# Four cache pages side by side on 32 partitions each, in the decode attention of a hybrid layer

## The chip, the cores and the metric

The kernel runs on one core of a Trainium2 chip. The metric is the time on the device of one execution, in microseconds (us): 3503.11 us before the change, the median of three runs (3503.08 to 3503.35). The core has five engines with a queue of instructions each: PE (TensorE, matrix products), DVE (VectorE), ACT (ScalarE), POOL (GpSimd) and SP (SyncE, which here only issues transfers). Transfers between the chip's memory (HBM) and the on-chip memory of 128 partitions are carried out by 16 DMA engines as packets, one for each contiguous run of bytes. SP and ACT issue theirs to queues of their own (q1 and q10 in the profile), POOL its gathers by index to q0; the 16 engines serve all of these queues.

## What is computed

One layer of a hybrid decoder for two groups: a prompt of 1024 tokens (eight tiles of 128) and eight samples of one new token each. Each token goes through latent attention beside a short gated convolution, and then through a mixer that fetches 128 rows of 1024 numbers from each of two expert tables. All numbers are float32.

The part that the change touches is the attention of the samples over their past. Each sample has 2048 past keys, in 16 pages of 128 keys; a page table says where each page lies. A key has a latent of 256 numbers (`ckv`) and a rotary part of 64 (`krope`):

```
past_ckv = cache_ckv[l, page_table].reshape(dec_b, past, KV_RANK)
past_kr = cache_krope[l, page_table].reshape(dec_b, past, QK_ROPE)
keys_ckv = jnp.concatenate([past_ckv, ckv], axis=1)
keys_kr = jnp.concatenate([past_kr, kr], axis=1)
s = (einsum('bqhr,bkr->bhqk', q_lat, keys_ckv)
     + einsum('bqhp,bkp->bhqk', q_rope, keys_kr)) * SM_SCALE
p = softmax(where(mask, s, -inf))
o_lat = einsum('bhqk,bkr->bqhr', p, keys_ckv)
```

A sample's new token comes after all of its past, so the mask hides none of these keys, and neither the softmax nor the weighted sum depends on the order in which the keys stand.

## The kernel before

**Two streams.** The mixer is the long one. For each prompt tile, 128 slots are worked off in 32 groups of four: for every slot POOL issues two gathers (L1853), each fetching one 4 KB row of `expert_u` or `expert_v` for each of the 128 tokens, 512 KB in all, into one of eight places of `u_ring` or `v_ring`. DVE multiplies a `u_ring` place with the tokens (L1736), ACT applies a gelu (L1215) and makes weighted diagonal matrices (L1222), and PE adds up the `v_ring` rows (L924). POOL waits for a place to come free, by `u_free` and `v_free`, before it issues the next gather into it. Between two tiles ACT reloads `xn2_cur` with the next tile's tokens (L1235), in two DMAs that write 64 partitions each.

Around this, a plan written out at build time puts the stages of everything else, one or a few per group: the projections and the attention of later prompt tiles and then of the samples. The samples' stages lie in groups 193 to 249 of 256, 36 of them named `pages` (groups 201 to 230).

**The pages.** The 16 pages of a sample are worked off in four quarters of four. The stage `pages` n takes quarter q = n % 4 of sample b = n // 4:

- `page_turn` on PE waits until all DMAs of the quarter have landed (`pages_loaded[b % 2][q]`), then transposes the four pages, two blocks of latents (L861) and one of rotary keys (L862) for each, into PSUM; ACT and DVE copy them to `pages_T` (L1156, L1523, L1524).
- `page_scores` multiplies them with the queries of all samples (L839, L840), ACT copies the result (L1153), and `page_scores_turn` picks and turns sample b's scores (L852).
- Once a sample's four quarters are through, the softmax follows, and `page_values` (L878, L881, L883), two stages into the next sample, weighs the latents as they lie in their load buffer. Its end counts `page_pv`.

There are two sets of buffers. Odd samples use `work`, even ones `ckv_rows` and `ckvT` (free by then) for latents and `w_ukT` for rotary keys. In both, page n is the slab of 256 (or 64) numbers at place n, and its 128 keys lie on the 128 partitions.

**SP's queue.** SP issues in a fixed order: the latents of sample 0 early, during the stage before; then loads of the rope tables (`cos_t`, `sin_t`, 64 partitions each, L477 and L478), of weights and of the sample tokens (`x_t`, L458); then the rotary keys of sample 0; then both parts of samples 1 to 7. From sample 2 on it waits first for `page_pv` of sample b - 2, whose buffer it overwrites. For each page it reads the page number from the table (L533) and issues one DMA for latents (128 KB) and one for rotary keys (32 KB), both at L536. Then come the weights of the samples' remaining stages.

Of the kernel before, what the change touches and what calls it, by code (L numbers as in the profile page):

```python
# [26 lines left out]
P = 128  # L27
# [3 lines left out]
TILES = SEQ // P  # L31
# [8 lines left out]
KV = 256  # L40
# [31 lines left out]
QP = NPAGES // QUARTERS  # L72
# [188 lines left out]
def build(nc, a, out):  # L261

    with ExitStack() as ctx:
        def sb(name, shape, dt=F32):
            return ctx.enter_context(nc.sbuf_tensor(name, shape, dt))
# [44 lines left out]
        work = sb("work", [P, 5 * D])  # L310
# [41 lines left out]
        prompt_keys = [ckv_rows[:, :, :], ckvT[:, :, :].rearrange("p c (n r) -> p (c n) r", r=KV)]  # L352
        pages_kr = [w_ukT[:, :, :].rearrange("p h (n r) -> p (h n) r", r=ROPE),
                    work[:, NPAGES * KV:NPAGES * (KV + ROPE)].rearrange("p (n r) -> p n r", r=ROPE)]

        def page_rows(b, n):
            if b % 2:
                return work[:, n * KV:(n + 1) * KV]
            return prompt_keys[n // TILES][:, n % TILES, :]

        pages_T = rows_next[:, :, :].rearrange("p a b -> p (a b)")[:, 0:3 * 512].rearrange("p (c k) -> p c k", c=3)

        SPREAD = [W[0], W[1], W[2], W[3], W[4], mix_raw, o_lat, x_t[:, :]]
# [81 lines left out]
        def _(sp):  # L445
# [19 lines left out]
            r = 0  # L465
            for name in ("g_mix_norm", "g_q", "g_kv", "g_attn_out", "g_conv_out"):
                n = a[name].shape[1] // P
# [5 lines left out]
            def load_rope(u):  # L473

                after(sp, on.q_roped, UNITS[u][0])
                row, T = UNITS[u][0] * P, width(u)
                sp.dma_start(cos_t[:, 0:T], a["c_rope"][0, :, row:row + T]).then_inc(on.rope_loaded, 16)  # L477
                sp.dma_start(sin_t[:, 0:T], a["c_rope"][1, :, row:row + T]).then_inc(on.rope_loaded, 16)  # L478
# [53 lines left out]
            def load_page(b, n, what):  # L532
                page = sp.value_load(page_table_sb[0:1, b * NPAGES + n:b * NPAGES + n + 1], min_val=0,  # L533
                                     max_val=a["cache_ckv"].shape[1] - 1)
                for dst, src in what:
                    sp.dma_start(dst, a[src][0, bass.ds(page, 1)].rearrange("a k r -> k (a r)"))\  # L536
                        .then_inc(pages_loaded[b % 2][n // QP], 16)

            sp.wait_ge(on.olat_kept, TILES * H)  # L540
            sp.wait_ge(on.pages_table_loaded, 16)
            for n in range(NPAGES):
                load_page(0, n, [(page_rows(0, n), "cache_ckv")])
            load_rope(SAMPLE)
            load_unit_start(SAMPLE)
            for k in range(CONV, N_IN + WR):
# [5 lines left out]
            sp.wait_ge(on.conv_done, SAMPLE + 1)  # L552
            sp.wait_ge(on.conv_stored, 3 * 16)
            for n in range(NPAGES):
                load_page(0, n, [(pages_kr[0][:, n, :], "cache_krope")])
            for b in range(1, SB):

                if b >= 2:
                    sp.wait_ge(on.page_pv, b - 1)
                for n in range(NPAGES):  # L560
                    load_page(b, n, [(page_rows(b, n), "cache_ckv"), (pages_kr[b % 2][:, n, :], "cache_krope")])
            for k in range(N_IN + WR, PIECES):
                load_w(SAMPLE, k)

# [1387 lines left out]
```

## Time and profile before

| | |
|---|---|
| median of 3 runs | 3503.11 us |
| the profiled execution: time | 3499.09 us |
| the profiled execution: span from first to last instruction | 3497.3 us |
| mean granted TensorE clock, as a share of full speed | 0.842 |
| busy: PE, DVE, ACT, POOL | 71%, 65%, 23%, 65% |
| moved by DMA | 1279.47 MB, 366 GB/s on average |
| page stage (first to last `pages` stage) | about 2768 to 3158 us |

The page of the profile gives the busy time of each engine, the DMA queues with their packets, megabytes and share of the time of 16 engines, and the costliest lines. The view of windows gives the same sums for a stretch of time: busy time and count of instructions for each engine, the granted clock, the share of the DMA engines' time taken by packets, and the rate in GB/s. A share can come out slightly over 1, as the records of packets overlap a little. "Under 512 B", "under 2 KB" and "under 8 KB" count all packets below that size, the 4-byte ones that raise semaphores among them. SPq and ACTq are the queues of SP and ACT, where their DMAs are issued.

### The profile page before, as it was taken

The numbers are of one execution on the slowest core, as the hardware profiler recorded it, in microseconds if no ns is written. First come the engines' busy times: TensorE is split into PE (matmuls) and PEld (weight loads), VectorE is DVE, ScalarE is ACT, GpSimd is POOL, SyncE is SP. The second block draws the span as 40 slices with busy tenths as digits, with TensorE's granted clock in tenths as the row PEclk, the third lists the DMA queues.
The fourth block names the chain that finished last, engine by engine and source line by source line (L and its number), as shares of the span: only waits on it lengthen the run. The fifth ranks groups of instructions, "written<-read, shape, count | busy, mean of one in ns | idle before, by whom it ended". The sixth has DMA issues, their size and how long they took to land.

```text
span 3497.3 us, 38783 instructions
## 1 busy us (share of the span) xinstructions
PE 2499.0 (71%) x11520; PEld 1392.1 (40%) x11520; DVE 2279.7 (65%) x5456; ACT 812.6 (23%) x2057; POOL 2290.4 (65%) x2068
## 2 busy tenths in 40 slices
PE   7558775878764598777744978778656978776764
PEld 6425442645531264445311644445213534332321
DVE  3585586655688756657898466558796455554774
ACT  2112212232211212322112223322112122221111
POOL 0366575655657776676777767666676676657675
PEclk8779887999987799899877999889876798987777
DMA  6699999988999999999999999999999999999998
GB/s 237 224 399 363 347 410 334 388 313 298 372 351 372 370 404 371 352 366 412 409 371 372 397 392 349 331 374 410 405 371 379 388 387 370 368 323 394 411 409 338
DMA packets 368936, 1279.47 MB, mean 366 GB/s; under 512 B 59372, under 2 KB 77974, under 8 KB 353368
## 3 DMA queue, kind: packets, MB, share of 16 engines
q0 software_dynamic: 297216, 1082.26, 80.7%
q1 hardware_dynamic: 62324, 168.67, 12.6%
q10 hardware_dynamic: 9188, 26.05, 2.3%
q8 instruction: 95, 1.56, 0.2%
q14 instruction: 113, 0.93, 0.1%
HBM read 1262.31 MB, written 13.48 MB: 365 GB/s over the span
## 4 chain that ended last, share of the span: by engine, by line
DVE 37%; PE 30%; DMA 15%; issue 8%; ACT 4%; SPq 3%; POOL 2%; DVEq 0%; ACTq 0%; POOLq 0%
DVE u_ring L1736 15%; PE acc L924 9%; PE front L586 8%; DMA u_ring<-in_expert_u,pick_cur 7%; DMA v_ring<-in_expert_v,pick_cur 4%; PE front L802 3%; DVE si_u L1603 2%; SPq L536 2%; DVE sv L1602 2%; PE front L711 2%; DVE work L1603 2%; DMA w_ukT<-in_cache_krope 2%; POOL u_ring L1853 1%; DVE work L1602 1%; PE front L734 1%
## 5 line engine op out<-in xcount | busy, mean ns | idle before, releaser
L924 PE MATMUL acc<-v_ring,diag 128*64 128x512 f32 x4096 | 1161.5, 716 | 612.6 <-ACT diag L1222 352.9
L1853 POOL DMA_INDIRECT v_ring<-in_expert_v,pick_cur x1024 | 1133.2, 1107 | 606.1 <-PE acc L924 333.0
L1853 POOL DMA_INDIRECT u_ring<-in_expert_u,pick_cur x1024 | 1140.5, 1114 | 575.4 <-issue 295.1
L1736 DVE CUSTOM_DVE_ANT_0 u_ring<-u_ring,xn_cur 128x1024 f32<-128x1024 f32 x1024 | 1210.8, 1222 | 315.4 <-DMA u_ring<-in_expert_u,pick_cur 309.3
L924 PEld LDWEIGHTS acc<-v_ring,diag 128*64 128x64 f32 x4096 | 340.7, 163 | 1316.6 <-issue 856.9
L1222 ACT ACTIVATE diag<-ident,wgt 128x64 f32<-128x64 f32 x1024 | 272.3, 337 | 797.6 <-DVE wgt L1742 727.9
L586 PE MATMUL front<-work,w_ring 128*128 128x256 f32 (+2 forms) x1536 | 308.1, 343 | 31.0 <-DVE mo L1337 17.1
L586 PE MATMUL front<-mo,w_ring 128*128 128x256 f32 (+2 forms) x1536 | 300.5, 337 | 0.0
L586 PEld LDWEIGHTS front<-work,w_ring 128*128 128x128 f32 x1536 | 250.5, 200 | 83.0 <-issue 29.3
L1215 ACT ACTIVATE gelu<-dots 128x4 f32<-128x4 f32 x256 | 52.5, 205 | 962.9 <-DVE dots L1736 962.8
L586 PEld LDWEIGHTS front<-mo,w_ring 128*128 128x128 f32 x1536 | 255.3, 201 | 23.4
L802 PE MATMUL front<-w_ring,work 128*128 128x256 f32 (+1 forms) x512 | 119.0, 394 | 22.4 <-DVE work L1568 16.7
L1602 DVE MAX8 sv<-work 128x8 f32<-128x128 f32 (+1 forms) x252 | 72.6, 288 | 75.9 <-ACT work L1200 29.9
L802 PEld LDWEIGHTS front<-w_ring,work 128*128 128x128 f32 (+1 forms) x512 | 93.5, 185 | 52.8 <-DVE work L1568 18.5
L1523 DVE COPY rows_next<-front 128x512 f32<-128x512 f32 x32 | 22.1, 691 | 139.7 <-PE front L862 139.7
L1215 ACT ACT_TABLE_LOAD x81 | 103.9, 1283 | 1.5
L734 PE MATMUL front<-work,ckv_rows 128*128 128x128 f32 x560 | 80.3, 307 | 28.7 <-DVE work L1507 25.2
L734 PEld LDWEIGHTS front<-work,ckv_rows 128*128 128x128 f32 x560 | 74.8, 217 | 40.8 <-DVE work L1507 29.5
L1736 DVE DVE_READ_ACCUMULATOR2_ANT dots<- 128x1 f32 x1024 | 84.0, 82 | 0.0
L711 PE MATMUL front<-ckvT,rows_next 128*128 128x512 f32 (+3 forms) x176 | 74.1, 546 | 7.0 <-DVE q_ro L1424 5.9
L1493 DVE SCALAR_TENSOR_TENSOR work<-low_keys,small,front 128x512 f32<-128x512 f32 (+3 forms) x44 | 26.6, 635 | 70.6 <-PE front L712 70.6
L1603 DVE FIND_INDEX8 si_u<-sv,work 128x8 uint32<-128x128 f32 (+1 forms) x252 | 71.5, 284 | 0.6 <-issue 0.6
(303 smaller groups left out, 2374.6 us busy)
## 6 DMA issues: line engine op xcount, KB each, us to landing
w_ring<-in_w_pieces SPq DMA_DIRECT2D x112, 1024.0 KB, 8.4
u_ring<-in_expert_u,pick_cur POOLq DMA_INDIRECT x1024, 10.5
v_ring<-in_expert_v,pick_cur POOLq DMA_INDIRECT x1024, 9.7
x_t<-in_x_prompt SPq DMA_DIRECT2D x16, 512.0 KB
v_ring<-in_w_pieces SPq DMA_DIRECT2D x8, 1024.0 KB, 12.0
work<-in_cache_ckv SPq DMA_DIRECT2D x64, 128.0 KB, 7.9
xn_cur<-scratch ACTq DMA_DIRECT2D x14, 512.0 KB, 9.8
scratch_x<-rows_next ACTq DMA_DIRECT2D x8, 512.0 KB, 6.6
```

The costliest lines, as they stand in the source:

```text
L536: sp.dma_start(dst, a[src][0, bass.ds(page, 1)].rearrange("a k r -> k (a r)"))\
L586: last = nc.tensor.matmul(dst, w[:, k, c0:c0 + m], x_chunks(k // 4)[:, (k % 4) * T:(k % 4 + 1) * T], start=(k == 0), stop=(k == DC - 1))
L711: nc.tensor.matmul(dst, q_lat[:, c, h, :], ckvT[:, c, ks], start=(c == 0), stop=False)
L734: last = nc.tensor.matmul(F[4][:, c * P:(c + 1) * P], ckv_rows[:, j, c * P:(c + 1) * P], W[1][:, j * P:(j + 1) * P], start=(j == 0), stop= ...
L802: last = nc.tensor.matmul(dst, mixed[i][:, k * T:(k + 1) * T], w[:, k, :], start=(k == 0), stop=(k == DC - 1))
L924: last = nc.tensor.matmul(acc[rows, half, :], diag[:, s % RING, :], v_ring[:, s % RING, half * 512:half * 512 + 512], start=(s < 2), stop= ...
L1215: nc.scalar.activation(gelu[:, g * G:(g + 1) * G], dots[:, g * G:(g + 1) * G], ACT.Gelu).then_inc(on.gelu_done, 1)
L1222: nc.scalar.activation(diag[:, s % RING, :], ident2[:], ACT.Copy, scale=wgt[:, s:s + 1]).then_inc(on.diag_made, 1)
L1602: own(v.max(best, scores), held=True)
L1603: last = v.max_index(index[:, 8 * r:8 * r + 8], best, scores)
L1736: v.tensor_tensor_reduce(u_ring[:, slot, :], u_ring[:, slot, :], xn2_cur[:, block_of(r), :], 1.0, 0.0, ALU.mult, ALU.add, dots[:, g * G + ...
L1853: pool.indirect_dma_start(ring[:, slot, :], None, a[table][0], bass.IndirectOffsetOnAxis(ap=pick, axis=0)).then_inc(loaded[slot], 16)
```

## The change

A page of latents is 128 rows of 1 KB, one after the other in memory, and was written row by row to 128 partitions. Now four consecutive rows go to one partition: a page takes 32 partitions and the room of four slabs, and the four pages of a quarter lie side by side, page i of the quarter on partitions 32 i to 32 i + 31. The same is done with the rotary keys. The new `page_block` and `kr_block` give the places to write to; `page_rows` stays, and a slab that it gives now holds every fourth key of each of the four pages. Since latents and rotary keys are permuted alike, a quarter is used only when whole, and the order of keys doesn't matter, nothing else changes: not the readers, the number or order of DMAs, the waits, nor the buffers.

```diff
+        def page_block(b, n):
+
+            q, i = divmod(n, QP)
+            part = slice(i * P // QP, (i + 1) * P // QP)
+            if b % 2:
+                return work[part, q * QP * KV:(q + 1) * QP * KV]
+            rows = prompt_keys[q * QP // TILES][part, q * QP % TILES:q * QP % TILES + QP, :]
+            return rows.rearrange("p n r -> p (n r)")
+
+        def kr_block(b, n):
+
+            q, i = divmod(n, QP)
+            return pages_kr[b % 2][i * P // QP:(i + 1) * P // QP, q * QP:(q + 1) * QP, :].rearrange("p n r -> p (n r)")
...
                 for dst, src in what:
-                    sp.dma_start(dst, a[src][0, bass.ds(page, 1)].rearrange("a k r -> k (a r)"))\
+                    sp.dma_start(dst, a[src][0, bass.ds(page, 1)].rearrange("a (m j) r -> (a m) (j r)", j=QP))\
                         .then_inc(pages_loaded[b % 2][n // QP], 16)
...
-                load_page(0, n, [(page_rows(0, n), "cache_ckv")])
+                load_page(0, n, [(page_block(0, n), "cache_ckv")])
...
-                load_page(0, n, [(pages_kr[0][:, n, :], "cache_krope")])
+                load_page(0, n, [(kr_block(0, n), "cache_krope")])
...
-                    load_page(b, n, [(page_rows(b, n), "cache_ckv"), (pages_kr[b % 2][:, n, :], "cache_krope")])
+                    load_page(b, n, [(page_block(b, n), "cache_ckv"), (kr_block(b, n), "cache_krope")])
```

Here P is 128, QP 4 (pages in a quarter), TILES 8, KV 256.

## Rows read from the trace of the kernel before

**Rows 1.** The page: busy time, and two DMA queues (packets, MB, share).
```profile
PE 2499.0 (71%) x11520; PEld 1392.1 (40%) x11520; DVE 2279.7 (65%) x5456; ACT 812.6 (23%) x2057; POOL 2290.4 (65%) x2068
...
q0 software_dynamic: 297216, 1082.26, 80.7%
q1 hardware_dynamic: 62324, 168.67, 12.6%
```

**Rows 2.** Windows of the whole core, columns in the first line.
```profile
core 0: us, PE busy (x) PEld busy (x) DVE busy (x) ACT busy (x) POOL busy (x), PEclk, DMA share, GB/s
2492.00:2532.00 40.00, 21.73 (x70) 7.68 (x72) 36.48 (x95) 7.37 (x21) 27.75 (x25) 0.77 1.03 409
...
2635.00:2641.00 6.00, 2.95 (x8) 1.08 (x10) 5.55 (x16) 3.74 (x7) 4.47 (x6) 0.62 1.02 256
...
2761.00:2764.00 3.00, 0.36 (x2) 0.40 (x3) 1.23 (x2) 0.70 (x3) 2.39 (x3) 0.80 1.01 361
...
3085.00:3090.00 5.00, 3.53 (x26) 2.62 (x25) 1.03 (x2) 1.17 (x2) 0.00 (x0) 1.00 0.44 130
...
2768.00:3158.00 390.00, 312.83 (x1687) 151.98 (x1686) 194.75 (x409) 101.58 (x250) 255.46 (x224) 0.86 0.99 361
3158.00:3490.00 332.00, 203.82 (x892) 85.62 (x884) 212.33 (x515) 56.60 (x177) 229.81 (x219) 0.77 1.00 398
```

**Rows 3.** DMA queues, 2492 to 2532 us: packets, MB, share.
```profile
q0 software_dynamic: 4484, 16.32, 102.5%
```

**Rows 4.** DMA queues, 2456 to 2475 us (latents of sample 0).
```profile
DMA packets 3302, 7.52 MB, mean 396 GB/s; under 512 B 362, under 2 KB 1835, under 8 KB 3301
...
q0 software_dynamic: 1651, 6.01, 80.7%
```

**Rows 5.** DMA queues, 2996 to 3024 us (page stage).
```profile
DMA packets 5225, 11.00 MB, mean 393 GB/s; under 512 B 1738, under 2 KB 2904, under 8 KB 5224
...
q0 software_dynamic: 2608, 9.50, 86.8%
q1 hardware_dynamic: 2616, 1.49, 17.6%
```

**Rows 6.** Reload of xn2_cur: its issue, and DMA queues 2635 to 2641 us.
```profile
L1235 ACTq DMA_DIRECT2D xn_cur<-scratch x2: 605/613/621, 2630.4 to 2631.1; - x2
...
q0 software_dynamic: 221, 0.83, 55.1%
q10 hardware_dynamic: 197, 0.70, 46.8%
```

**Rows 7.** Rope tables: issue, and DMA queues 509.5 to 512.5 us.
```profile
502.66 0.58 SPq L478 DMA_DIRECT2D sin_t<-in_c_rope  x1
...
DMA packets 394, 1.08 MB, mean 360 GB/s; under 512 B 62, under 2 KB 153, under 8 KB 394
...
q0 software_dynamic: 271, 0.99, 93.1%
```

**Rows 8.** DMA queues, 2768 to 3158 us (the page stage).
```profile
q0 software_dynamic: 32899, 119.80, 81.2%
q1 hardware_dynamic: 34560, 18.89, 16.5%
q10 hardware_dynamic: 432, 1.57, 1.4%
```

**Rows 9.** Timeline of SP's queue (start, duration), two pages of sample 4.
```profile
2938.33 0.34 SPq L536 DMA_DIRECT2D ckv_rows<-in_cache_ckv  x1
...
2939.94 0.34 SPq L536 DMA_DIRECT2D ckv_rows<-in_cache_ckv  x1
```

**Rows 10.** Waits of PE, 2768 to 3158 us: total, times, longest.
```profile
PE front L861 <- DMA w_ukT<-in_cache_krope: 29.7, 9, 7.4
PE front L861 <- DMA work<-in_cache_krope: 16.0, 5, 7.4
```

## The prediction

> **What bounds the kernel now.** I read the page first: no compute engine is busy for more than 71% of the span, while the expert gathers take 80.7% of what 16 DMA engines have and the queue of SP and its like 12.6% more [rows 1]. Then the windows. Where nothing but gathers is under way the DMA share is 1.03 at 409 GB/s, the most that this kernel moves. The page stage (attention of the eight samples over their cache pages, 2768 to 3158 us) has a share of 0.99 but 361 GB/s, and after it the rate is 398. PE is busy for 313 of its 390 us, DVE for 195 [rows 2]. So the DMA engines are the bound, and in the page stage something makes them less productive. Every DMA microsecond added or saved there moves all that follows, as the gathers stay the bound to the end.
>
> Last I took the price of each kind of packet out of windows in which the DMA engines never idle, as (window x 16 engines) less what the others took.
> - Gathers alone: 40 us x 16 = 640 us of engine time for 16.32 MB, or 3984 packets of 4096 bytes: 0.161 us each [rows 3].
> - Key rows of sample 0 (1 KB packets, 128 partitions): 19 x 16 = 304, less 6.01 MB of gathers (1467 x 0.161 = 236), leaves 68 for 1835 - 362 = 1473 packets: 0.046 each [rows 4].
> - Page stage in full flow, 1 KB and 256 B packets mixed: 28 x 16 = 448, less 9.50 MB (2319 x 0.161 = 373), leaves 75 for 2616 packets of q1: 0.029 each [rows 5]. In the stage q1 has 34560 packets for 240 page DMAs, 144 a DMA (128 and 16 for the semaphore); a page (two DMAs) has 288, or 8.3 us of engine time [rows 8].
>
> **What the change does, part by part.**
> 1. *Fewer, larger packets.* A page of latents goes from 128 packets of 1 KB to 32 of 4 KB, its rotary keys from 128 of 256 B to 32 of 1 KB. At the wide prices a page would cost 32 x 0.161 + 32 x 0.046 = 6.6 us instead of 8.3; over 128 pages and 16 engines that is -1.7 x 8 = -13.6 us.
> 2. *Fewer partitions per DMA.* Each page DMA now writes 32 partitions instead of 128. No DMA of before does just that, but two kinds write 64, and both spoil the rate. The reload of `xn2_cur` (L1235, two DMAs of 64 partitions, 4 KB packets) [rows 6] drops it to 256 GB/s with the engines never idle [rows 2]: 6 x 16 = 96 us, less 0.83 MB of gathers (203 x 0.161 = 32.7), leaves 63.3 for 0.70 MB, 171 packets: 0.37 each, 2.3 times the wide price [rows 6]. The rope tables (64 partitions, 1 KB packets) cost 3 x 16 = 48, less 0.99 MB (242 x 0.161 = 38.9), 9.1 for 153 - 62 = 91 packets: 0.100 each, 2.2 times [rows 7]. An 8-row load of the sample tokens leaves 361 GB/s behind it [rows 2], so fewer partitions are at least no better. I bound a page between no penalty, 6.6 us, and the rope and reload prices, 32 x 0.37 + 32 x 0.100 = 15.0 us. The nearest rows are the 64-partition ones; as these were dense bursts and the page packets come thinner, I take a little over twice, 2.05 x 6.6 = 13.5 us. Against 8.3 that is +5.2 x 128 / 16 = +42 us (+54 at the upper price, +39 at exactly twice).
> The Trainium skill ("SBUF — State Buffer", "Door 1: The DMA port swizzle (why `[64,N]` ≈ `[32,N]`)") states that partitions 0 to 31 reach the same eight of the sixteen SBUF ports as 0 to 63, and 64 to 127 the other eight, so 32 rows go as slowly as 64. The trace agrees for 64 (0.37 against 0.161 us) and has no 32-row DMA; by the rule the sum is mine, without it only the -13.6 us of part 1 would stand. Its "DMA: Bandwidth & Descriptors" ("Why a DMA increments its semaphore by 16 and not by 1") has a DMA of 32 rows still spread over 16 engines; no row here shows one.
> 3. *Pages land sooner.* Queues take turns packet by packet: in full flow 2608 packets of the gathers' queue stand beside 2616 of q1 [rows 5]. A quarter (four pages) is 4 x 288 / 16 = 72 packets an engine, each behind a gather packet: 72 x (0.161 + 0.029) = 13.7 us. SP issues a page in 1.61 us, a quarter in 6.4 [rows 9]. After the change a quarter has 24 packets an engine (8 + 8 and 8 for semaphores), at the doubled price 4 x 13.5 / 16 + 24 x 0.161 = 7.3 us, near what SP needs to issue it. PE now waits for pages in 14 turns for 45.7 us [rows 10]; behind it the ring fills, the gathers stop, and slices like 3085 to 3090 move 130 GB/s [rows 2]. I expect most of these waits gone. What they are worth is the idle time of the DMA engines, not 45.7 us: 390 x 16 = 6240, less gathers 119.80 MB (29248 x 0.161 = 4709), page packets 34560 x 0.029 = 1002, q10's 1.57 MB (256 slow at 0.37 and 127 at 0.161, 115), instructions some 19, leaves 395 / 16 = 25 us [rows 8]. The stage after it, without pages, runs 2.7% under 409 GB/s [rows 2], which over 390 us is 10; so 15 us come back, between 0 and 22.
> 4. *No other step moves.* Same number of DMAs, instructions, semaphores and waits; the keys of a quarter are only permuted alike in latents and rotary keys. SP's issue is paid per DMA (0.33 us), so it stays at 1.61 us a page. The 16 latent DMAs of sample 0 stand in the 128 pages of part 2. PE and DVE keep their cover: 313 us of PE work in a stage of some 415.
>
> **The sum.** +42 - 15 = +27 us on the profiled execution's 3499.1 us, 3526; its median of runs is 4 us above, so 3530.
>
> **Rivals.**
> - *A, narrow writes cost double (forecast).* 3530; by its bounds +39 - 22 = +17 to +54 - 4 = +50, so 3520 to 3553.
> - *B, no penalty: faster.* The page DMAs alternate, two pages on the lower and two on the upper 64 partitions, and come thinner than a burst; if what is buffered absorbs the crowding, only parts 1 and 3 count: -13.6 - 15 = -29, 3474 (3465 to 3485). It decides the sign when a page costs less than 8.3 + 15 / 8 = 10.2 us, that is, under about 1.5 times the wide price. Against it: the rope burst brings a mere 128 KB, as one page does, and pays in full.
> - *C, half the penalty.* A page at 10 us: +14 - 15, 3502 (3495 to 3512).
> - *D, the packets don't merge.* If rows of 1 KB remained and only narrowed, a page would cost 2 x 8.3: +66 and no waits saved, 3569. Against: rows that are contiguous on both sides already move as 4 KB packets in the gathers.
>
> **How the numbers follow.** A 0.56, C 0.14, B 0.26, D 0.04. This kernel's measurement tells about 0.2%, 7 us, from no change. Slower: A, D and the upper fifth of C, 0.62; faster: B and a little of C, 0.28; same: 0.10. A's own range is 3520 to 3553. Eight in ten need A, C and half of B: 3474 to 3554 leaves out the lower half of B (0.13), D and a thin tail of A. Cases of both signs are in it, because the penalty for 32 partitions is read from 64-partition DMAs.
>
> **What will show it.** Packets of q1 in the page stage fall from 34560 to about a third (11520, 48 a DMA): right for part 1, and D is out. A window of the page stage with a DMA share over 1 and under 350 GB/s, where gathers and 4 KB page packets should give 400: A. The same window near 400 GB/s: B. Waits of PE L861 on page DMAs under 15 us: part 3. The page stage grows from 390 to about 415 us, and the stages before and after it keep their length. I am wrong if the stage shrinks, or if it grows while the DMA share falls below 0.95, for then something other than the DMA engines would set it.

## The result

After the change the kernel takes 3527.2 us, the median of its runs, beside 3503.2 us for the kernel before: the ratio is 1.0064, with a 95% interval of 1.0051 to 1.0078. It is 24 us slower. (One of the six runs of after, at 3613 us, was in a slower state, and the ratio leaves it out.) The profiled execution takes 3527.2 us, its span is 3524.7.

The windows of after, of the page stage, of the stage behind it, and of 20 us in the page stage. The columns are those of [rows 2].

```profile
core 0: us, PE busy (x) PEld busy (x) DVE busy (x) ACT busy (x) POOL busy (x), PEclk, DMA share, GB/s
3070.00:3090.00 20.00, 11.91 (x57) 5.29 (x55) 7.78 (x18) 4.65 (x10) 11.63 (x11) 0.91 1.04 286
2776.00:3190.00 414.00, 321.77 (x1689) 149.21 (x1688) 197.14 (x409) 101.59 (x250) 262.59 (x229) 0.84 1.03 343
3190.00:3520.00 330.00, 205.67 (x888) 87.24 (x884) 210.95 (x517) 59.24 (x180) 227.92 (x214) 0.76 0.99 396
```

The page stage has grown from 390 to 414 us, and it moves 343 GB/s instead of 361 although the DMA share has risen from 0.99 to 1.03 [rows 2]: the engines are busy all the time and get less done. The stage behind it is as fast as before (396 against 398).

The DMA queues of after in the page stage, 2776 to 3190 us (packets, MB, share):

```profile
q0 software_dynamic: 33259, 121.12, 84.6%
q1 hardware_dynamic: 11520, 18.89, 16.8%
q10 hardware_dynamic: 433, 1.57, 1.4%
```

The packets of q1 are 11520 for the same 240 DMAs and the same 18.89 MB, a third of the 34560 before [rows 8]: the rows did join to 4 KB and 1 KB. But a third of the packets takes more of the engines (16.8% of 414 us against 16.5% of 390).

The price of a page, as in the prediction, is the time of DMA engines that one page takes, summed over the 16. From 3070 to 3090 us of after:

```profile
q0 software_dynamic: 1072, 3.90, 70.0%
q1 hardware_dynamic: 1070, 1.80, 33.7%
q8 instruction: 1, 0.02, 0.4%
q14 instruction: 1, 0.01, 0.1%
```

20 x 16 = 320 us of engine time, less 952 gather packets at 0.161 (153) and 1.6 for q8 and q14, leaves 165 for 1.80 MB. A page is 0.164 MB, so this is 11.0 pages, 15.0 us each. By [rows 5] the same sum gives 8.2 before. The 27 windows of 20 us in this stage of after without idle engines lie between 13.4 and 16.4, with a median of 14.8 (a table further down has those of all runs).

The sum charges the whole loss to the pages, but the records show that the gathers bear part of it. A packet of q0 (those for semaphores included) takes 1.025 x 640 / 4484 = 0.146 us where gathers are alone [rows 3], 0.868 x 448 / 2608 = 0.149 in the page stage of before [rows 5], and 0.70 x 320 / 1072 = 0.209 in this window. The gathers are the same in both kernels.

The early latents of sample 0 alone, 2455 to 2472 us of after, answer to [rows 4]:

```profile
DMA packets 1620, 4.81 MB, mean 283 GB/s; under 512 B 459, under 2 KB 459, under 8 KB 1608
...
q0 software_dynamic: 809, 2.95, 63.0%
q1 hardware_dynamic: 810, 1.85, 40.9%
```

272 us, less 720 gather packets (116) and 12 weight packets of 8 KB (about 4), leaves 152 for 1.75 MB or 427 packets: 0.356 us for a 4 KB packet to 32 partitions, beside 0.161 for one of a DMA over 128 and 0.37 for the reload over 64 [rows 6]. For the 16 DMAs that is 182 us of engine time against 94 before, 5.5 us of the 8.2 by which the first transpose of the pages starts later (2791.4 us against 2783.2).

The waits of PE in the page stage of after (total, times, longest):

```profile
PE acc L938 <- DMA v_ring<-in_expert_v,pick_cur: 62.4, 21, 9.7
PE front L866 <- ACT low_keys L1167: 11.0, 3, 9.7
PE acc L938 <- ACT diag L1236: 5.7, 2, 4.6
PE front L875 <- DMA w_ukT<-in_cache_krope: 3.9, 2, 2.2
PE front L875 <- DMA work<-in_cache_krope: 3.0, 1, 3.0
```

L875 is L861 of before, L938 is L924. The waits for pages have fallen from 45.7 us [rows 10] to 6.9. In their place PE waits 62.4 us for the gathers, against this in the page stage of before:

```profile
PE acc L924 <- DMA v_ring<-in_expert_v,pick_cur: 12.5, 8, 3.4
```

### The profile page after: what moved, and what is told of

Its sections match the earlier page's. It is cut to its first block, busy times and chain, and to the rows that moved or that the text cites. A ratio compares the mean times of both kernels' runs of the same rounds, so it can differ in the third digit from the quotient of the medians.

```text
span 3524.7 us, 38783 instructions
## 1 busy us (share of the span) xinstructions
PE 2522.5 (72%) x11520; PEld 1394.0 (40%) x11520; DVE 2280.6 (65%) x5456; ACT 812.7 (23%) x2057; POOL 2294.4 (65%) x2068
## 4 chain that ended last, share of the span: by engine, by line
DVE 35%; PE 31%; DMA 18%; issue 8%; ACT 4%; POOL 4%; DVEq 0%; SPq 0%; ACTq 0%; POOLq 0%
DVE u_ring L1750 14%; PE acc L938 10%; DMA u_ring<-in_expert_u,pick_cur 9%; PE front L600 8%; DMA v_ring<-in_expert_v,pick_cur 7%; PE front L816 3%; POOL u_ring L1867 2%; DVE si_u L1617 2%; PE front L725 2%; DVE sv L1616 2%; DVE work L1617 1%; POOL v_ring L1867 1%; DVE work L1616 1%; PE front L748 1%; DVE work L1661 1%
## 5 line engine op out<-in xcount | busy, mean ns | idle before, releaser
L938 PE MATMUL acc<-v_ring,diag 128*64 128x512 f32 x4096 | 1195.0, 733 | 660.2 <-ACT diag L1236 336.5
L938 PEld LDWEIGHTS acc<-v_ring,diag 128*64 128x64 f32 x4096 | 348.0, 166 | 1387.1 <-issue 932.6
L1236 ACT ACTIVATE diag<-ident,wgt 128x64 f32<-128x64 f32 x1024 | 272.3, 337 | 793.3 <-DVE wgt L1756 727.9
```

The lines of the kernel that those rows point to most:

```text
L938: last = nc.tensor.matmul(acc[rows, half, :], diag[:, s % RING, :], v_ring[:, s % RING, half * 512:half * 512 + 512], start=(s < 2), stop= ...
L1236: nc.scalar.activation(diag[:, s % RING, :], ident2[:], ACT.Copy, scale=wgt[:, s:s + 1]).then_inc(on.diag_made, 1)
```

## The experiments

Two theories. T: packets of a DMA that writes a narrow range of partitions crowd on few destinations and hold up the engines, gathers included. R: the large page packets take every second turn from the gathers, and it is their lateness that costs the time. The price of a page, from windows in which the engines never idle, tells whether the narrow range costs engine time; the times tell whether that decides. The times need one remark. They come from five measurements, in each of which the kernel before ran too. In two, the first and that of e9 to e11, it takes 3501 to 3503 us. In the other three (e1 to e4, e5 to e8, e12), each on another chip, it took 3635 to 3640, with larger scatter. Only e9 to e11 test the time where the DMA engines are the bound; what the times on the other chips say is weighed under e1 and e5 and after e11.

The expectations speak of a page stage of 376 us in the kernel before. That is its length from the first transpose of a page (2783.2 us) to the last product of `page_values` (3158.8). By the same marks it is 399 us in after; the 390 and 414 above start some 15 us earlier.

**e1 and e5: every fourth partition.** The same packets, spread over 128 partitions.

```diff
-            part = slice(i * P // QP, (i + 1) * P // QP)
+            part = slice(i, P, QP)
...
-            return pages_kr[b % 2][i * P // QP:(i + 1) * P // QP, q * QP:(q + 1) * QP, :].rearrange("p n r -> p (n r)")
+            return pages_kr[b % 2][i:P:QP, q * QP:(q + 1) * QP, :].rearrange("p n r -> p (n r)")
```

> As after the change, but page i of a quarter goes to every fourth partition (i, i + 4, ..., i + 124) instead of 32 adjacent ones. Packets are the same (32 of 4 KB, 32 of 1 KB a page), the destinations spread over all 128 partitions. Theory T (packets for a narrow range of partitions crowd on few destinations and cost double): the crowding is gone, only the saving by larger packets (-13.6 us) and by pages landing sooner (-15 us) is left: 3474 us, 3465 to 3485, and the page stage runs near 400 GB/s. Rival R (the large page packets take every second turn of the DMA engines from the gathers, whose lateness costs the 24 us): nothing of that changes, 3527 us.

Measured on the first of the slower chips: 3651.7 us against 3634.9, ratio 1.0046 (1.0025 to 1.0067). As a ratio to before, T expected 0.992 and R 1.007, so the time is nearer to R. The price of a page had fallen (5.7 to 7.7 us in the three windows with hardly any idle time), but the time hadn't. The DMA engines were idle for part of the page stage, whose DMA share is 0.92 (columns of [rows 2]):

```profile
2875.00:3296.00 421.00, 332.71 (x1682) 158.75 (x1683) 195.55 (x411) 100.64 (x250) 251.13 (x230) 0.82 0.92 335
```

Over the whole of e1, ACT's longest waits include these, for which the trace names no cause (the first was 1.1 us in before):

```profile
ACT diag L1236 <- issue: 372.7, 89, 19.4
ACT gelu L1229 <- issue: 242.2, 50, 16.0
```

So in e1 the DMA engines aren't the bound of the stage, and the price of a page doesn't set the time. A second run came to another chip of that kind.

> The kernel of e1 (each page on every fourth partition) once more, because on the chip of the first four runs the kernel before took 3635 us instead of 3503 and waits that no semaphore ended had grown on ACT and PE. The price of a page there was 6.8 us of engine time, against 15.0 in the kernel after. T: where the kernel before takes about 3503, this one takes 3474 (3465 to 3485), and its page stage is shorter than the 376 us of before. If the lower price is lost to something else, it is no faster than the kernel before.

Measured: 3656.5 us against 3639.5, ratio 1.0054 (1.0019 to 1.0088). The condition of the expectation, 3503 for before, wasn't met. The DMA share of the page stage is 0.93, and on these two chips the version is no faster, and slightly slower.

**e2 and e12: narrow, but small packets.** Rows m, m + 32, m + 64 and m + 96 go to one partition, so none join.

```diff
-                    sp.dma_start(dst, a[src][0, bass.ds(page, 1)].rearrange("a (m j) r -> (a m) (j r)", j=QP))\
+                    sp.dma_start(dst, a[src][0, bass.ds(page, 1)].rearrange("a (j m) r -> (a m) j r", j=QP))\
```

> The range of 32 partitions as after the change, but partition m of a page's range takes the rows m, m + 32, m + 64, m + 96, so that no two rows join and the packets are those of before (128 of 1 KB, 128 of 256 B a page). T: narrow packets cost double at 0.046 and below too, a page 2 x 8.3 = 16.6 us of engine time, +66 us against before and no waits saved: 3569 us, 3545 to 3580. R: small packets take little from a gather's turn, as before: 3503 us.

Measured: 3676.2 us against 3634.9, ratio 1.0118 (1.0080 to 1.0155). DMA queues of e2, 3038 to 3058 us:

```profile
q0 software_dynamic: 1647, 6.02, 88.1%
q1 hardware_dynamic: 1645, 0.93, 16.9%
```

320 - 1470 x 0.161 = 83 us for 5.68 pages: 14.7 us a page. The packets are those of before and the turns too (1647 and 1645), yet the page costs 1.8 times as much. R has nothing that could do this. Once the range is narrow, the size of the packets hardly changes the price of a page: 15.0 us in after and 14.7 here, or 14.8 and 15.2 as medians of all such windows.

> The kernel of e2 (32 partitions a page, packets of 1 KB and 256 B) once more, for its time where the kernel before takes about 3503: the fourth corner beside 3501 (spread, small packets), 3524 (narrow, large) and 3471 (spread, large). T: its page costs 15 us of engine time as in e2, 6.7 more than before; over 128 pages and 16 engines +54 us, of which the 25 us in which the engines stood idle in the page stage of before can take up to half: 3530 to 3557. R: 3503.

Measured: 3669.6 us against 3637.9, ratio 1.0089 (1.0059 to 1.0119), again on a chip where before took 3638, so the expected time can't be tested. A page costs 16.0 us there (median of 25 windows). The version is slower than before on both chips, by 41 us (e2) and 32 us (e12).

**e3: a step of two within 64 partitions.**

```diff
-            part = slice(i * P // QP, (i + 1) * P // QP)
+            part = slice(i // 2 * 64 + i % 2, i // 2 * 64 + 64, 2)
```

> As after the change, but with a step of two partitions: pages 0 and 1 of a quarter take the even and the odd ones of the lower 64, pages 2 and 3 those of the upper 64. It tells a range of 64 and a step apart from the spread over 128. T, with the 64-partition reloads as its case: 64 adjacent partitions are as crowded as 32, so 3527 us as after the change (3518 to 3536). If it is the number of partitions in reach that counts in proportion, it would halve the penalty: about 3500. R: 3527 too.

Measured: 3656.4 us against 3634.9, ratio 1.0039 (1.0006 to 1.0073). DMA queues of e3, 3062 to 3082 us:

```profile
q0 software_dynamic: 1281, 4.66, 75.5%
q1 hardware_dynamic: 924, 1.57, 28.0%
```

320 - 1138 x 0.161 - 2 = 135 us for 9.58 pages: 14.0 us a page (median 14.3). Twice the range, within one half, gives back almost nothing.

**e4: lower and upper half in turns.**

```diff
-            for n in range(NPAGES):
+            ORDER = [q * QP + i for q in range(QUARTERS) for i in (0, 2, 1, 3)]
+            for n in ORDER:
```

> As after the change, with the pages of a quarter issued in the order 0, 2, 1, 3, so that lower and upper 64 partitions take turns from page to page. T with engines that stand still while they wait: each DMA by itself is as crowded as ever, 3527 us (3518 to 3536). T with enough buffering to even out two neighbouring pages: the crowding shrinks by up to half, about 3510. R: 3527.

Measured: 3654.0 us against 3634.9, ratio 1.0056 (1.0027 to 1.0085). DMA queues of e4, 3110 to 3130 us:

```profile
q0 software_dynamic: 1160, 4.23, 71.0%
q1 hardware_dynamic: 1055, 1.81, 32.5%
```

320 - 1033 x 0.161 - 2 = 152 us for 11.0 pages: 13.7 us a page, a relief of about 1 us against after (medians 13.8 and 14.8). So two DMAs in a row are hardly evened out, which was rival B's condition.

**e6 and e7: one part alone.** e6 loads only the latents in blocks, e7 only the rotary keys, with the other part as before.

```diff
-                    sp.dma_start(dst, a[src][0, bass.ds(page, 1)].rearrange("a (m j) r -> (a m) (j r)", j=QP))\
+                    sp.dma_start(dst, (a[src][0, bass.ds(page, 1)].rearrange("a (m j) r -> (a m) (j r)", j=QP) if src == "cache_ckv" else a[src][0, bass.ds(page, 1)].rearrange("a k r -> k (a r)")))\
...
-                    load_page(b, n, [(page_block(b, n), "cache_ckv"), (kr_block(b, n), "cache_krope")])
+                    load_page(b, n, [(page_block(b, n), "cache_ckv"), (pages_kr[b % 2][:, n, :], "cache_krope")])
```

> Only the latents go to blocks of 32 partitions as 4 KB packets; the rotary keys are loaded as before (128 partitions, 256 B). Latents and rotary keys of a page then belong to different keys, so this kernel's attention of the samples is not the reference's; no work is left out. T: a page costs 32 x 0.36 = 11.5 for latents and 2.4 for rotary keys, 13.9 us of engine time, and takes +45 less about 10 for pages that land sooner: 3538 less the rest, near 3530 (3515 to 3545). If the rotary keys carry the penalty, about 3500.

> Only the rotary keys go to blocks of 32 partitions as 1 KB packets; the latents are loaded as before (128 partitions, 1 KB). As in the run before, latents and rotary keys of a page belong to different keys, and no work is left out. T: a page costs 5.9 + 32 x 0.11 = 9.4 us of engine time, +1.1 x 8 = +9 us, less a few for fewer packets to wait behind: near 3505 (3497 to 3515).

Measured: e6 3657.5 us and e7 3627.3, both against 3639.5; ratios 1.0050 (1.0015 to 1.0084) and 0.9973 (0.9942 to 1.0004). DMA queues of e6, 3110 to 3130 us, and of e7, 3022 to 3042 us:

```profile
q0 software_dynamic: 1467, 5.34, 82.4%
q1 hardware_dynamic: 1464, 1.18, 22.6%
```

```profile
q0 software_dynamic: 1668, 6.08, 80.7%
q1 hardware_dynamic: 1821, 1.54, 23.5%
```

By the same sum 15.2 us a page for e6 (median of its windows 15.9, with wide scatter) and 8.6 for e7. The latents carry the penalty. The rotary keys in blocks cost about as much as before; that their fewer packets make up for the crowding is my reading, and no run separates the two.

**e8: spread, halfway in size.** Two rows to each of 64 partitions, every second one over all 128.

```diff
-            part = slice(i * P // QP, (i + 1) * P // QP)
+            first = q * QP + i // 2 * 2
...
-                return work[part, q * QP * KV:(q + 1) * QP * KV]
+                return work[i % 2:P:2, first * KV:(first + 2) * KV]
...
-                    sp.dma_start(dst, a[src][0, bass.ds(page, 1)].rearrange("a (m j) r -> (a m) (j r)", j=QP))\
+                    sp.dma_start(dst, a[src][0, bass.ds(page, 1)].rearrange("a (m j) r -> (a m) (j r)", j=2))\
```

> Halfway in size and still spread: two rows of a page to each of 64 partitions, with a step of two over all 128, packets of 2 KB and 512 B. T (spread decides, then packet size): a page costs between the 8.3 us of 1 KB packets and the 6.8 of 4 KB, near 7.3, and pages land somewhat sooner: 3485 us (3475 to 3495), though it writes 64 partitions like the reloads that cost double. If the count of partitions decides and not their place, it costs like those, 13 us a page, near 3525.

Measured: 3644.8 us against 3639.5, ratio 1.0048 (1.0014 to 1.0082). The one window of e8 without idle engines, 2918 to 2938 us:

```profile
q0 software_dynamic: 2011, 7.30, 91.5%
q1 hardware_dynamic: 727, 0.75, 10.7%
```

320 - 1782 x 0.161 - 1 = 32 us for 4.58 pages: 7.0 us a page. Two more windows, at a share of 1.02, give 8.6 and 8.7, in which some idle time is counted as cost. It writes 64 partitions a DMA, as the reloads of `xn2_cur` do at 0.37 us a packet, and a page comes nowhere near the 13 us of that price. So it isn't the count of partitions that decides but whether they are spread over both halves. The expected time, 3485 us, was meant for a chip where before takes 3503 us and can't be tested here.

**e9, e10, e11: before, after and every fourth partition on one chip.** The same three kernels once more, unchanged.

> The kernel before, unchanged, for a profile from the chip of this job. On the two chips of e1 to e8 it took 3635 and 3639 us, 3.8% more than the 3503 of the first measurement. If it takes about 3503 here, the waits that no semaphore ends (372 us ahead of ACT's diagonal matrices in e1) are gone, and the DMA share of its page stage is near 0.99; if about 3635, its page stage is longer than 376 us too, and its DMA share there well under 0.99.

> The kernel after, unchanged. T: a page costs 15.0 us of engine time as before (14.5 to 15.5) wherever it runs. Where the kernel before takes 3503: +24 us. Where it takes 3635, its DMA engines are idle for longer, and part of the dearer pages falls into that idle time: between 0 and +24 us.

> The kernel of e1 and e5 (every fourth partition) beside the kernel before on one chip, with both profiles. The price of a page stays at 6.9 us of engine time against 8.3. Where the kernel before takes 3503 and the DMA engines are the bound: 3474 (3465 to 3485) by T; by R (large packets take the gathers' turns, and late gathers cost the time) no faster than 3503. Where it takes 3635: e1 and e5 were 0.5% slower than before, and the profiles of the page stages, side by side, should show whether the gathers come later there although the engines have less to do.

The engines were the bound here: in e9 the DMA share of the page stage is 1.00, and ACT's nameless waits are gone. Measured, with the kernel before at 3501.1 us: e9 3502.1 (ratio 1.0005, 0.9995 to 1.0015), e10 3524.1 (1.0068, 1.0055 to 1.0082), e11 3470.7 (0.9922, 0.9908 to 0.9936). e11 beats both kernels, by 30 and 53 us. Page stages of e9 and e10, then of e11 20 us in the page stage and the whole of it:

```profile
2770.00:3161.00 391.00, 321.65 (x1678) 154.81 (x1677) 194.26 (x407) 101.49 (x250) 259.95 (x228) 0.84 1.00 362
...
2774.00:3188.00 414.00, 320.82 (x1696) 148.24 (x1698) 197.15 (x409) 101.99 (x251) 259.01 (x225) 0.84 1.02 341
...
2942.00:2962.00 20.00, 16.84 (x90) 7.84 (x90) 14.55 (x35) 8.76 (x21) 13.44 (x13) 1.00 1.03 405
2775.00:3135.00 360.00, 296.52 (x1650) 136.98 (x1652) 195.06 (x407) 101.73 (x249) 264.98 (x226) 0.91 1.02 390
```

The DMA queues of e11 in the same two stretches:

```profile
q0 software_dynamic: 1745, 6.35, 79.5%
q1 hardware_dynamic: 980, 1.73, 23.1%
```

```profile
q0 software_dynamic: 32820, 119.49, 85.5%
q1 hardware_dynamic: 11520, 18.89, 14.2%
```

Ten and a half pages cost 320 - 1550 x 0.161 - 1 = 69 us, 6.6 us each. e11 has the 11520 page packets of after among about as many of the gathers (32820 and 33259); only the partitions differ. A DMA still has 32 rows, so a cause that goes with the number of rows, such as fewer engines at work on one DMA, is out as well. The stage is 360 us long, 54 less than in after, and the engines have (15.0 - 6.6) x 115 pages / 16 = 60 us less to do. R forecast no less than 3503 us for it and is out as the cause of the 24 us, T stands.

The records say who pays. From e11 to after the packets of q1 take 0.168 x 6624 - 0.142 x 5760 = 295 us more of engine time in the stage, those of q0 0.846 x 6624 - 0.855 x 5760 = 679 more, of which some 70 are for 439 packets more. About two thirds of the penalty falls on the gathers.

The price of a page in all windows of 20 us in the page stages (8 us apart) that have a DMA share of 1.025 or more, no reload, and at least 0.6 MB on q1, with the mean record of a q0 packet in them:

| kernel | partitions of one DMA | packets (latents) | windows | us a page: median (all) | q0 packet, us |
|---|---|---|---|---|---|
| before, e9 | 128 | 1 KB | 21, 22 | 8.2, 8.2 (7.8 to 13.3) | 0.150, 0.150 |
| e7, rotary keys alone | 128 (latents) | 1 KB | 13 | 8.5 (8.3 to 9.6) | 0.153 |
| e11 | every 4th of 128 | 4 KB | 21 | 6.5 (6.3 to 7.8) | 0.146 |
| after, e10 | 32 adjacent | 4 KB | 27, 27 | 14.8, 14.6 (12.8 to 16.7) | 0.186, 0.186 |
| e2, e12 | 32 adjacent | 1 KB | 32, 25 | 15.2, 16.0 (12.4 to 20.6) | 0.174, 0.177 |
| e6, latents alone | 32 adjacent (latents) | 4 KB | 35 | 15.9 (5.9 to 19.2) | 0.180 |
| e3 | every 2nd of 64 | 4 KB | 28 | 14.3 (13.2 to 15.5) | 0.176 |
| e4 | 32 adjacent, halves in turns | 4 KB | 29 | 13.8 (12.8 to 16.8) | 0.179 |

e1, e5 and e8 have two, none and one such window.

What the traces don't show is where two packets meet, as no record names an engine or a destination. That the place is the way into one half of the partitions is inferred from e3, e4, e8 and e11; no version put a page on a few adjacent partitions of each half. Not settled either: why e1, e5 and e8 were half a per cent slower than before on chips where before takes 3635 to 3640 us. The narrow e3, e4 and e6 were slower by as much (0.4 to 0.6%), though their pages cost twice as much, and e7, which keeps the 1 KB latents, was not slower. So on those chips the spread brought nothing, and large latent packets went with the loss, wide or narrow. There R may have a part, as late gathers could count where other waits rule. No run isolates this, and neither before nor after has a profile from such a chip.

## Why the prediction was right

The forecast was 3530 us, rival A, with 3520 to 3553 as its own range; measured were 3527.2 and 3524.1.

- *The bound.* Right, on the chips where before takes 3501 to 3503 us. The DMA share of the page stage is 1.03 in after and 1.02 in e11, and its length follows the engine time of the pages in both directions.
- *Part 1, packets merge.* Right: 11520 packets in the stage. The wide price, worked out as 6.6 us a page, is 6.6 in e11.
- *Part 2, narrow writes.* The mechanism was right, the size too small: I took 13.5 us a page, measured are 15.0, so the term is (15.0 - 8.3) x 8 = +54 us and not +42. This was my upper bound, from the dense bursts [rows 6, 7]. I had chosen less because page packets come thinner; that discount was the error.
- *Part 3, pages land sooner.* Right in kind: 6.9 us of waits where I said under 15. The size was too small as well. The stage of after has 414 x 16 = 6624 us of engine time; gathers 29570 x 0.161 = 4761, pages 115.3 x 15.0 = 1730, q10 115 and instructions 20 fill it. So nothing is idle, and all 25 us came back, not 15 (half a microsecond in the price of a page would be 3.6 us here). In e11 the same sum (5760 - 4697 - 761 - 115 - 20 = 167) leaves 10 us idle, which is what I had expected for a stage without page waits: the crowded engines of after had none even of those.
- *The sum.* +54 - 25 = +29 against the +28 of the profiled executions and the +24 of the medians. The two errors of 12 and 10 us cancel; that the forecast came within 3 us was luck. The range didn't need it, as +54 was its upper price. (It ends at +54 - 4, though part 3 allowed that nothing comes back; with 0 it would end at 3557.)
- *Part 4.* Mostly right. SP needs 0.32 us for each DMA instead of 0.33, and the longest issue of a latent DMA fell from 2.6 us to 0.4; no row shows that this moved anything. The stage behind took 330 us instead of 332. The page stage starts 8 us later, of which 5.5 are the early latents, counted in the 128 pages; the rest is not traced.
- *The rivals.* B fell with its condition: e4 found the order of halves to matter little, and the window that should have shown 400 GB/s shows 286. But its time, 3474, is close to that of e11 (3470.7), for it was the price of this change without the narrow range. D fell by the packet count, C by the price. For D, e2 and e12 are the kernel: slower than before by 41 and 32 us, less than the +66 that I gave it, but on the slower chips. Their price, 15.2 and 16.0 where I had 16.6, explains little of that, and the rest is not tested where the DMA engines are the bound.
- *The Trainium skill's rule* ("SBUF — State Buffer", "Door 1: The DMA port swizzle (why `[64,N]` ≈ `[32,N]`)"), that 32 partitions reach the same eight ports as 64, agrees with the runs: 0.356 us a packet for 32 and 0.37 for 64, and 14.0 us a page in e3, within 64 partitions, against 15.0 in after.

## What to carry to other kernels

Where the DMA engines are the bound, the price of a load depends on where its partitions lie more than on the size of its packets: merging rows to 4 KB saved 1.6 us a page when they were spread (e11), and putting the same packets on 32 adjacent partitions cost 8.4 more. If rows must go to few partitions, take every fourth over all 128, which is one slice. This paid only where before takes 3501 us (30 us); where it takes 3635 to 3640 it did not. And look in the trace of before for DMAs with narrow ranges: the two reloads of `xn2_cur`, unchanged in all of these kernels, show the same price, and their window of 6 us at 256 GB/s gave the upper bound that was then measured.

## What the runs showed of the hardware

- A DMA to 32 adjacent partitions costs 0.356 us of engine time for a 4 KB packet, against 0.161 over 128 partitions. The gathers beside it pay: their own packets take 0.209 us instead of 0.149, and the rate of all falls from 409 to 286 GB/s. I hadn't expected that the packet's size would hardly count: 15.0 us a page in 4 KB and 1 KB packets, 14.7 in 1 KB and 256 B.
- 32 rows with a step of four are cheaper than 128 adjacent ones (6.6 us a page in e11, 8.2 before), and 64 with a step of two cost 7.0 in the one full window of e8. A step within one half of the partitions doesn't help (14.0 in e3).
- The same kernel takes 3501 to 3503 us in two measurements and 3635 to 3640 in three, on three other chips. In profiles of its variants from the latter, ACT waits hundreds of microseconds for something that the trace doesn't name (372.7 us at L1236 in e1, against 1.1 in before).
